# Moving the branch stage's input tiles by 16 and 48 bytes against the 128-byte grid

## The reference

```python
h = rmsnorm(x, g_pre_mix)
m_qk, m_v, m_o, m_if, a_q, a_k, a_v, merge = split(h @ w_in)
i_pre, f_pre = split(m_if + b_gates)
hm = head_rmsnorm(mlstm_chunkwise(m_q, m_k, m_v, i_pre, log_sigmoid(f_pre)), m_head_norm)
y_m = (sigmoid(m_o) * hm) @ w_branch_m
ha = head_rmsnorm(diff_attention(a_q, a_k, a_v, lam), a_head_norm) * (1.0 - lam_init)
y_a = ha @ w_branch_a
g_m, g_a = split(sigmoid(merge))
x = x + rmsnorm((g_m * y_m + g_a * y_a) @ w_out, g_post_mix)
# then the gated MLP: rmsnorm, @ w_up, causal conv, gelu(gate) * val, @ w_down, rmsnorm
```

## Time and profile before

| | |
|---|---|
| runs before | 1875.78, 1876.03, 1876.25 us |
| profiled execution, its own time | 1875.96 us |
| its span, first to last instruction | 1874.2 us |
| TensorE clock granted, mean | 0.997 |
| TensorE (PE) busy | 1842.5 us, 98% |
| weight loads (PEld) | 1741.8 us, 93% |
| VectorE (DVE) | 1097.0 us, 59% |
| ScalarE (ACT) | 895.9 us, 48% |
| GpSimd (POOL) | 78.3 us, 4% |
| DMA | 351.35 MB, mean 187 GB/s |

### The profile page before, as it was taken

The page is one execution under the profiler, slowest core; times in us unless marked ns, Lnnn a source line. Parts: engine busy times, 40 slices in busy tenths (PEclk is TensorE's granted clock), DMA queues, the critical chain, the costliest instruction groups (busy, mean ns, idle before and its releaser), DMA issues.

```text
span 1874.2 us, 35840 instructions
## 1 busy us (share of the span) xinstructions
PE 1842.5 (98%) x13774; PEld 1741.8 (93%) x13774; DVE 1097.0 (59%) x1287; ACT 895.9 (48%) x1159; POOL 78.3 (4%) x103
## 2 busy tenths in 40 slices
PE   6999999999999999999999998999999999999998
PEld 6999999999999999999999887999999999988886
DVE  5565556655665565545554556666666676755555
ACT  6444445444544454444434445555455445544443
POOL 4700000000000000000000001000000000000000
PEclk9999999999999999999999999999999999999999
DMA  6655655555555555565565653666666665565553
GB/s 212 201 182 171 191 180 175 175 188 178 176 178 182 179 178 180 180 194 195 186 197 194 253 193 125 199 194 191 199 190 192 192 197 183 198 215 190 190 191 135
DMA packets 166294, 351.35 MB, mean 187 GB/s; under 512 B 12916, under 2 KB 13517, under 8 KB 165581
## 3 DMA queue, kind: packets, MB, share of 16 engines
q1 hardware_dynamic: 165005, 344.40, 56.9%
q10 hardware_dynamic: 848, 4.79, 0.7%
q0 software_dynamic: 368, 1.09, 0.3%
HBM read 348.12 MB, written 2.12 MB: 187 GB/s over the span
## 4 chain that ended last, share of the span: by engine, by line
issue 60%; PE 39%; DVE 0%; POOL 0%; POOLq 0%; ACT 0%; DVEq 0%; ACTq 0%
PE ps L1136 12%; PE ps L1138 12%; PE ps L1137 12%; PE ps L1198 1%; PE ps L1271 1%; PE ps L1248 0%; POOLq L470 0%; PE ps L1206 0%; POOL stat L471 0%; PE ps L1247 0%; PE ps L1254 0%; DVE gm L861 0%; DVE h L833 0%; DVE xn L833 0%; POOL hm_hi L459 0%
## 5 line engine op out<-in xcount | busy, mean ns | idle before, releaser
L837 DVE TENSOR_TENSOR w_lo<-raw,w_hi 128x1024 fp32r<-128x1024 f32 x638 | 780.4, 1229 | 668.8 <-ACT w_hi L541 667.5
L541 ACT ACTIVATE w_hi<-raw 128x1024 fp32r<-128x1024 f32 x640 | 677.8, 1062 | 782.6 <-PE ps L1138 618.6
L1136 PE MATMUL ps<-h,w_hi 128*128 128x256 f32 x3200 | 886.3, 277 | 0.0
L1137 PE MATMUL ps<-h,w_hi 128*128 128x256 f32 x3200 | 883.6, 276 | 0.0
L1138 PE MATMUL ps<-h,w_lo 128*128 128x256 f32 x3200 | 883.6, 276 | 0.0
L1137 PEld LDWEIGHTS ps<-h,w_hi 128*128 128x128 f32 x3200 | 600.7, 188 | 0.6
L1136 PEld LDWEIGHTS ps<-h,w_hi 128*128 128x128 f32 x3200 | 600.6, 188 | 0.6
L1138 PEld LDWEIGHTS ps<-h,w_lo 128*128 128x128 f32 x3200 | 600.6, 188 | 0.0
L1311 PE MATMUL ps<-w_hi,ks_hi 128*128 128x512 f32 x448 | 176.7, 394 | 0.3 <-DVE ks_lo L833 0.2
L1315 PE MATMUL ps<-w_lo,ks_hi 128*128 128x512 f32 x448 | 175.0, 391 | 0.0
L1311 PE MATMUL ps<-w_hi,ks_lo 128*128 128x512 f32 x448 | 139.5, 392 | 0.0
(11 more groups left out here) (166 smaller groups left out, 1381.6 us busy)
## 6 DMA issues: line engine op xcount, KB each, us to landing
raw<-in_w_in SPq DMA_DIRECT2D x288, 512.0 KB, 3.5
raw<-in_w_up SPq DMA_DIRECT2D x176, 512.0 KB, 4.3
raw<-in_w_down SPq DMA_DIRECT2D x88, 512.0 KB, 4.7
raw<-in_w_branch_m SPq DMA_DIRECT2D x32, 512.0 KB, 4.7
raw<-in_w_branch_a SPq DMA_DIRECT2D x32, 512.0 KB, 4.7
raw<-in_w_out SPq DMA_DIRECT2D x32, 512.0 KB, 4.7
x<-in_x ACTq DMA_DIRECT2D x1, 2048.0 KB, 11.5
gm<-in_x SPq DMA_DIRECT2D x3, 512.0 KB, 6.6
```

The source lines that it names most:

```text
L541: return nc.scalar.activation(out_ap, in_ap, ACT.Copy, scale=scale)
L837: nc.vector.tensor_tensor(in_lanes(w_lo, slot, lanes), raw_halves(slot), in_lanes(w_hi, slot, lanes).bitcast(F32), ALU.subtract).then_inc( ...
L1136: nc.tensor.matmul(out_ap, stat_hi, mov_hi, start=start, stop=False, skip_group_check=True)
L1137: nc.tensor.matmul(out_ap, stat_hi, mov_lo, start=False, stop=False, skip_group_check=True)
```

## The change

hm_hi and hm_lo become two views into one tensor hm that is 128 bytes longer than both together, and begin 4 words (16 bytes) into it; ha_hi and ha_lo likewise in a tensor ha, 12 words (48 bytes) into it. The views have the same shape as the tensors before. hm and ha are each a multiple of 128 bytes long, so all tensors behind them lie 128 or 256 bytes higher and at the same place modulo 128; those allocated after `mix.close()` (x1, act, gpost) don't move at all. Modulo 128 hm's tiles now begin at 80 and ha's at 112. No instruction is added, removed or moved in its queue.

```diff
         gm = sb("gm", [P, KT, T], stack=mix)
-        hm_hi = sb("hm_hi", [P, KT, T], F32R, stack=mix)
-        hm_lo = sb("hm_lo", [P, KT, T], F32R, stack=mix)
-        ha_hi = sb("ha_hi", [P, KT, T], F32R, stack=mix)
-        ha_lo = sb("ha_lo", [P, KT, T], F32R, stack=mix)
+        hm = sb("hm", [P, 2 * KT * T + 32], F32R, stack=mix)
+        ha = sb("ha", [P, 2 * KT * T + 32], F32R, stack=mix)
+        (hm_hi, hm_lo), (ha_hi, ha_lo) = (
+            [part[:, at + i * KT * T:at + (i + 1) * KT * T].rearrange("p (k t) -> p k t", t=T) for i in range(2)]
+            for part, at in ((hm, 4), (ha, 12)))
         heads = ExitStack()
```

## The result

The changed kernel takes 1884.59 us (median of 6 runs, 1883.50 to 1886.61) against 1876.33 us before (6 runs): 0.42% slower, ratio 1.0042 with a 95% interval of 1.0032 to 1.0053. That lies in the stated range of 1870.5 to 1887.2 us, but it isn't the case that I held for the likeliest. Its own range, 1875.5 to 1877.5 us, is missed by 7 us.

The account below looks back on a forecast made before the run. TensorE was taken to bound the kernel, never idle in the branch stage. To 1875.96 us came +0.6 for 1536 matmuls touching one more line, other terms 0, giving 1876.6 us; range 1870.5 to 1887.2 us.

Parts of the forecast that it names:

- the case that I held for the likeliest: Branch-stage matmuls run at the same rate or one cycle more: 1876.6 us, own range 1875.5 to 1877.5, chance 0.42.
- the two cases that they are named after: Branch-stage matmuls: every touched line paid whole, 1886.9 us; half of the faster case, one of hm and ha, 1870.9 us.
- What bounds the kernel: In the branch stage TensorE has no idle time, so each nanosecond per matmul moves the kernel's end by as much.
- +0.6 us: Branch stage's 1536 matmuls with hm or ha moving: one cycle, 0.42 ns, each for touching 17 lines in place of 16.
- the row of v's tiles: Value product: v's pieces begin inside 64-byte lines yet pay no surcharge, 0.20 us per entry; called weak support for +0.6.
- the two reads meet: Branch-stage matmuls slow when moving and stationary reads share a 64-byte half of 128: +5.1 us, up to +10.2; chance 0.21.
- A touched line is paid whole: Branch-stage matmuls pay 17 lines x 17 cycles, 120.4 ns each: +10.9 us, chance 0.17.
- Faster: Branch-stage matmuls: a start inside a line hides the surcharge, -10.2 us (1865.8) or half, -5.1 (1870.9); chance 0.20.
- level isn't always dear: 512-column float32r matmuls, both operands level at 0, pay no more than one cycle per line; held against the reads meeting.
- The gates: Gates' product, 48 matmuls with hm stationary, now 16 bytes from h modulo 128: 0 taken, between -0.3 and +0.3 us.
- What would show it: Start distances of hm and ha: 113.7 ns forecast, wrong if either is off 113.3 by over 2.4; h's must stay.
- The writers and the memset: ScalarE's and VectorE's 64 tiles of hm and ha, and the memset: nothing expected; 10% dearer tiles, 3 us, would be hidden.

## Why the prediction was right or wrong, point by point

**The range:** it held by luck. Its upper end was taken from the case of whole lines, which the runs refute, and what it had to cover was a loss by placement for which my sum had nothing. Its ends also stand 0.3 and 0.4 us outside the two cases that they are named after (1886.9 and 1870.9 us), without a reason given.

**What bounds the kernel:** right. TensorE had no idle time in the stage in any of the kernels, so each nanosecond per matmul came through to the end, and the copies of ScalarE and VectorE gave none of it back.

**The price of the change, "+0.6 us":** this step failed; measured are 8.3 us, of which 7.3 in the stage. I took the row of v's tiles as the nearest one, although I had called it weak: those tiles are read at half the rate, and a stream with slack may hide a conflict between two streams. One cycle for a 17th line may be about right as a size (0.5 to 0.7 ns are left with both operands moved), but it was not the term that counts. That is the distance between moving and stationary operand, which the sum put at nothing: 5.9 ns for each matmul of hm and 2.3 for each of ha. The two rows that did bear on it, and the earlier trace rows, I had read and given 0.21. They should have been the forecast: they were the only rows of 256-column float32r matmuls in which place or timing of the operands differs, and both were dear.

**The rival "the two reads meet":** right in its place and in that the position of the two operands to each other decides, since moving the weights along takes most of the loss away and moving them alone brings it. That reads meet inside the chip is not shown. Its two sizes were wrong and in the wrong order: 1.7 ns for hm and 5.0 for ha forecast, 5.9 and 2.3 measured. The model of overlapping halves of 128 bytes falls three times: the period is at least 256, as the exchange of ha's slow and fast slots shows; 4 and 8 bytes cost as much as 16; and one distance has two rates. Its upper time, 1886.2 us, was nearer than its central 1881.1.

**"A touched line is paid whole", 1886.9 us:** nearer to the time, at 2.3 us, than the central case of any other rival, and false. With both operands moved 17 lines are touched at 113.8 to 114.0 ns, not 120.4.

**"Faster":** no. No kernel had any 256-column float32r stretch below 113.3 ns.

**" show that level isn't always dear":** true, and modulo 256 it fits. There both operands are level modulo 256; the even slots of the row form are level modulo 128 only and take 232.7 ns.

**The gates:** I took 0, between -0.3 and +0.3. Once the clock is back, their matmuls take 118.2 ns and not 120.0, which is -0.1 us for the 48; the +0.5 us of the profile is the granted clock of 0.50. The kernel with the longer slots and hm unmoved has it too (clock 0.50 from 21 to 23 us, 6.76 us for the product). Nor is the -0.1 us a matter of addresses alone: with both operands of the branch stage moved, hm stands in the gates as in the change, and they take 120.0 ns. So the 120.0 of the earlier trace rows isn't the price of level operands alone either. The h matmuls behind them cost +0.3 us. That a stretch can slow the next one was in no term of the sum, though the earlier trace rows is such a case. It is 1.0 us in the stage.

**What would show it:** by my own sign the prediction is wrong, for hm's distance of 119.3 ns is 6.0 off 113.3 (the mean of ha, 115.6, is 2.3 off and would have passed). The signs for the meeting of reads, near 115 with hm and 118 with ha, came out the other way round. And I had written that if h's own distance changes, the cause isn't the alignment of hm and ha. It did change, to a mean of 115.0 ns, and goes back to 113.3 when ha alone is put back: that sign was false, because a stretch can depend on the one before.

**The writers and the memset:** nothing to be seen, as forecast (ScalarE's tiles of ha 470 ns before and after, VectorE's 474).

**Still open:** what sets a stretch into the one rate or the other. I have shown that two rates exist at one pair of addresses and that they depend on what ran before. That it is the phase between the stream of weights and the moving stream is the reading that fits, and not shown: the trace has the next weight load 3 to 4 ns behind the start of a matmul at 113.3 ns and 2 to 3 at 117.8, too coarse to tell. Why an alternation of the slots by 128 bytes brings the fast rate back isn't known either, nor which rule beyond the distance modulo 256 gives the four-unit pattern with only the weights moved.

## What to carry to other kernels

Where a float32r matmul stream is the bound, as here, place can matter for the pair of operands more than for one tile: measure the distance between starts for moving and stationary place modulo 256 bytes, and move both together or neither. Don't judge such an offset from a stretch in isolation; run it behind an interruption and behind another tensor, since the slow rate may be one that the stream keeps until something else interrupts it. And when a trace shows the same instruction at two rates, that row is the price list of a change of layout, before any row of a slower kind of instruction.

## What the runs showed of the hardware that was not expected

- 256-column float32r matmuls with fresh weights each have at least two steady rates at the same addresses, 113.3 and 117.8 ns, both at granted clock 1.00; with all ring slots alike the 4224 matmuls of the up projection stayed at 117.8, while stretches of the input projection took one or the other by what ran before them.
- 512-column ones take 226.7 ns with both operands at the same place modulo 256, 232.7 at 128 bytes apart and 227.9 at the same place when the units in between are 128 apart.
- Offsets of 4 and 8 bytes (119.0 and 120.7 ns) are worse than one of 48 (115.9).
- The gates' product, 5.8 us long, took 0.5 us more in the changed kernel (hm moved) and 0.9 more in the one with all slots alike (hm unmoved), where the granted clock was 0.50 at its start.
